# Two mixer phases of a transformer kernel take their inputs without the norm's root; the root meets each job's sums on the vector engine

## What is computed

```python
def rms_norm(x, gain, eps=1e-6):
    return x * lax.rsqrt(jnp.mean(x * x, axis=-1, keepdims=True) + eps) * gain

for l in range(2):
    x = x + 0.5 * swiglu(rms_norm(x, ffn1_norm[l]), ...)          # width 2816
    proj = rms_norm(x, mix_norm[l]) @ w_in[l]                     # 3328 columns
    y_rwkv = rwkv7_group(proj[..., :1792], ...)                   # p = p + mu * (p[t-1] - p[t]) first
    y_ret = retnet_group(proj[..., 1792:])                        # q, k rotary; v; gate silu(g)
    x = x + jnp.concatenate([y_rwkv, y_ret], -1) @ w_out[l]
    x = x + 0.5 * swiglu(rms_norm(x, ffn2_norm[l]), ...)
```

## Time and profile before

| | |
|---|---|
| median of 3 runs | 1433.2 us (1430.12 to 1433.49) |
| the profiled execution | 1431.56 us, of which its span 1429.7 us |
| PE busy | 1372.6 us, 96% |
| DVE busy | 986.9 us, 69% |
| ACT busy | 780.0 us, 55% |
| mean granted TensorE clock | 0.994 of full |

### The profile page before, as it was taken

The page is one execution under the profiler, slowest core; times in us unless marked ns, Lnnn a source line. Parts: engine busy times, 40 slices in busy tenths (PEclk is TensorE's granted clock), DMA queues, the critical chain, the costliest instruction groups (busy, mean ns, idle before and its releaser), DMA issues.

```text
span 1429.7 us, 28173 instructions
## 1 busy us (share of the span) xinstructions
PE 1372.6 (96%) x10866; PEld 1184.4 (83%) x10866; DVE 986.9 (69%) x1543; ACT 780.0 (55%) x1296; POOL 9.4 (1%) x23
## 2 busy tenths in 40 slices
PE   7998999999999999999999999999999999999997
PEld 7986887878888889877788887888879987788886
DVE  6977628877666677667766667766677855866665
ACT  6456546766555566335655555554565633655454
POOL 0000000000000000000000000000000000000000
PEclk9999999999999999999999999999999999999999
DMA  8732463145555554203565554655545401465551
GB/s 294 291 122 74 169 226 121 60 149 205 190 192 191 177 177 156 82 4 121 185 206 180 181 195 161 201 194 196 180 155 194 141 14 55 156 219 176 192 192 58
DMA packets 62789, 229.82 MB, mean 161 GB/s; under 512 B 7008, under 2 KB 7264, under 8 KB 62448
## 3 DMA queue, kind: packets, MB, share of 16 engines
q1 hardware_dynamic: 60912, 220.23, 45.8%
q0 software_dynamic: 1792, 8.37, 1.6%
HBM read 227.53 MB, written 1.05 MB: 160 GB/s over the span
## 4 chain that ended last, share of the span: by engine, by line
PE 83%; DVE 8%; ACT 6%; issue 2%; DMA 0%; DVEq 0%; SPq 0%; ACTq 0%
PE PS L793 23%; PE PS L1114 21%; PE PS L1134 16%; PE PS L1116 11%; DVE out_operands L2058 1%; PE PS L772 1%; PE PS L1322 1%; PE PS L1328 1%; DVE w_lo L2036 1%; PE PS L782 1%; DVE x_res L1962 1%; DVE w_lo L2318 1%; PE PS L1290 1%; ACT arena L1495 1%; PE PS L859 1%
## 5 line engine op out<-in xcount | busy, mean ns | idle before, releaser
L1114 PE MATMUL PS<-hT_both,w_hi 128*128 128x512 f32 x1376 | 489.9, 399 | 4.2 <-DVE w_lo L2318 4.2
L1116 PE MATMUL PS<-hT_both,w_lo 128*128 128x256 f32 x1376 | 386.1, 281 | 0.0
L1114 PEld LDWEIGHTS PS<-hT_both,w_hi 128*128 128x128 f32 x1376 | 258.5, 188 | 69.2 <-issue 3.4
L1116 PEld LDWEIGHTS PS<-hT_both,w_lo 128*128 128x128 f32 x1376 | 259.8, 189 | 3.0
L793 PE MATMUL PS<-hT_both,w_hi 128*128 128x256 f32 x1392 | 255.3, 286 | 2.3 <-DVE w_lo L2036 1.2
L793 PEld LDWEIGHTS PS<-hT_both,w_hi 128*128 128x128 f32 x1392 | 217.5, 192 | 6.5 <-issue 5.2
L2318 DVE TENSOR_TENSOR w_lo<-weight_ring,w_hi 128x1024 fp32r<-128x1024 f32 x176 | 207.1, 1218 | 2.4 <-ACT w_hi L1740 2.4
L793 PE MATMUL PS<-hT_both,w_lo 128*128 128x256 f32 x696 | 196.9, 283 | 0.0
L2324 DVE TENSOR_TENSOR w_lo<-weight_ring,w_hi 128x1024 fp32r<-128x1024 f32 x88 | 107.8, 1225 | 111.3 <-ACT w_hi L1749 111.3
L1740 ACT ACTIVATE w_hi<-weight_ring 128x1024 fp32r<-128x1024 f32 x176 | 175.4, 1045 | 0.0
L2036 DVE TENSOR_TENSOR w_lo<-weight_ring,w_hi 128x1024 fp32r<-128x1024 f32 x107 | 125.8, 1219 | 48.0 <-ACT w_hi L1518 47.8
(11 more groups left out here) (309 smaller groups left out, 1820.9 us busy)
## 6 DMA issues: line engine op xcount, KB each, us to landing
weight_ring<-in_stream SPq DMA_DIRECT2D x411, 512.0 KB, 4.4
norm_gain<-in_gains_in POOLq DMA_DIRECT2D x8, 512.0 KB, 4.2
consts<-in_csts POOLq DMA_DIRECT2D x1, 1864.0 KB, 9.4
arena<-in_taps_in SPq DMA_DIRECT2D x4, 384.0 KB, 3.4
arena<-in_bias_in POOLq DMA_DIRECT2D x1, 1152.0 KB, 12.4
x_res<-in_x_in SPq DMA_DIRECT2D x2, 512.0 KB, 3.7
lora<-in_lora_in POOLq DMA_DIRECT2D x2, 512.0 KB, 3.8
x_out<-yT SPq DMA_DIRECT2D x2, 512.0 KB, 2.7
```

Source lines behind the costliest of these rows:

```text
L1114: pe.matmul(PS[:, b, :], Wh[:, u, k, :], HT2[:, k], start=(k == 0), stop=(k == KT - 1), skip_group_check=True)
L1116: ins = pe.matmul(PS[:, b, 0:T], Wl[:, u, k, :], Hh[:, k, :], start=False, stop=(k == KT - 1), skip_group_check=True)
```

## The change

Mixers become "late" phases too. `late(n)` holds for them, so the seam into a mixer writes `x * gain` after each addition, and roots come behind the copies. PE makes the row of roots after J(0), in bank 7. In the mixer every sum but the two by token (J(9), J(10)) is multiplied by `root_row` on DVE as it leaves PSUM (`rooted`), in place of ACT's copy; ACT's copies of J(9) and J(10) take the root as their scale, and the gate's silu runs on SBUF behind DVE. In all late phases the first 128 tokens' root now comes before ACT's copies of the transposed inputs, the second's after them. In feed-forwards the PE waits for the gate's and the up projection's low parts one by one. In the even layer `fill(s)` stands ahead of `values(s - 2)`, and the sum of squares ahead of row k = 5.

```diff
-        ROOTS_AT = SPLIT_END + NTT * D + D
+        ROOTS_AT = ARENA - 2 * T - NTT
...
-            return n < len(PHASES) and PHASES[n][0].startswith("ffn")
+            return n < len(PHASES) and (PHASES[n][0].startswith("ffn") or PHASES[n][0] == "mix")
...
+            def row_of_roots(n, b):
+
+                pe.wait_ge(sem("roots_spread"), NTT * (late_before(n) + 1))
+                for t in range(NTT):
+                    ins = pe.matmul(PS[:, b, t * P:(t + 1) * P], cst("ones"), root_diag[:, t, :],
+                                    start=True, stop=True)
+                ins.then_inc(sem("root_row_made"), 1)
...
                     if s + 1 < n:
                         scores(s + 1)
+                    fill(s)
                     if s >= 2:
                         values(s - 2)
-                    fill(s)
...
-                    if k == 6:
+                    if k == 5:
                         pe.wait_ge(sem("convsq_made"), 1)
...
-                        if i == 0:
-                            pe.wait_ge(sem("gu_lo"), 2 * f0 + part + 1)
+                        pe.wait_ge(sem("gu_lo"), turns(it, 2 * FLOOP, 2 * (f0 + i) + part + 1))
...
                 J(0)
+                row_of_roots(n, 7)
                 J(1)
...
+            def late_root(n, t):
+                act.wait_ge(sem("x_made"), x_made_at(n - 1) + 2 * t + 2)
+                done.wait(done(act.activation(squares, X[:, t, :], ACT.Square, accum_out=stat[:, t:t + 1])))
...
-                act.activation(flat(qR), job_made(jb0, 7), ACT.Copy).then_inc(sem("job_out"), 1)
                 split_to(SPLIT["mix"][2][8])
...
-                act.activation(flat(kR), job_made(jb0, 8), ACT.Copy).then_inc(sem("job_out"), 1)
                 for n in (9, 10):
-                    act.activation(Vret[:, n - 9, :], job_made(jb0, n), ACT.Copy).then_inc(sem("job_out"), 1)
+                    split_to(SPLIT["mix"][2][n])
+                    act.wait_ge(sem("job_out"), jb0 + n)
+                    act.activation(Vret[:, n - 9, :], job_made(jb0, n), ACT.Copy, scale=stat[:, n - 5:n - 4])\
+                       .then_inc(sem("job_out"), 1)
...
                     act.preload_act_table_set("natural_log_exp_and_others")
+                    late_root(n, 0)
                     hT_split(n)
-                    late_roots(n)
+                    late_root(n, 1)
...
+                def rooted(n, dst):
+
+                    dve.wait_ge(sem("job_made"), jb0 + n + 1)
+                    dve.wait_ge(sem("root_row_copied"), late_before(ph) + 1)
+                    dve.tensor_tensor(dst, PS[:, job_bank("mix", n), :].rearrange("p (a t) -> p a t", a=2),
+                                      rep(root_row, 2), ALU.mult).then_inc(sem("job_out"), 1)
...
                     if n:
                         dve.wait_ge(sem("shift_made"), 7 * l + n)
+                    rooted(n, r[:, :, 1:T + 1])
+                    dve.wait_ge(sem("job_out"), jb0 + n + 1)
...
                 split_for(9)
+                rooted(7, qR)
                 dve.wait_ge(sem("decay_exp"), l + 1)
...
                 k = done(dve.tensor_tensor(flat(en), flat(en), flat(kh), ALU.mult))
                 done.wait(k)
 
+                rooted(8, kR)
...
+                dve.wait_ge(sem("job_out"), jb0 + 11)
+                rooted(11, gret[:, 0:2, :])
                 dve.tensor_tensor(flat(qW), flat(qR), cst("QW"), ALU.mult)
...
                     ins.then_inc(sem("st_masked"), 1)
+                rooted(12, gret[:, 2:4, :])
```

More of the change, by code:

```diff
@@ L1119, in gate_up @@
                     if i == 0:
[L1120 to L1124, removed]
+                        row_of_roots(n, 3)
                 def down(i, start, stop):
@@ L1141, in step @@
                 def step(i, it=None):
-                    if i:
-                        pe.wait_ge(sem("gu_lo"), turns(it, 2 * FLOOP, 2 * (f0 + i + 1)))
                     if f0 + i >= SS:
                         pe.wait_ge(sem("act_made"), turns(it, FLOOP, f0 + i - SS + 1))
-                    gate_up(i)
+                    gate_up(i, it)
                     if i == 0:
@@ L1490, in rstd, with root_row_copied @@
                        .then_inc(sem("rstd_made"), 1)
[L1492 to L1499, removed]
+            def root_row_copied(n, b):
+                act.wait_ge(sem("root_row_made"), late_before(n) + 1)
+                act.activation(root_row, PS[:, b, 0:T], ACT.Copy).then_inc(sem("root_row_copied"), 1)
+            def late_root(n, t):
+                act.wait_ge(sem("x_made"), x_made_at(n - 1) + 2 * t + 2)
+                done.wait(done(act.activation(squares, X[:, t, :], ACT.Square, accum_out=stat[:, t:t + 1])))
+                done.wait(done(act.activation(stat[:, 6 + t:7 + t], stat[:, t:t + 1], ACT.Ln,
+                                              scale=1.0 / D, bias=eps[:])))
+                act.activation(stat[:, 4 + t:5 + t], stat[:, 6 + t:7 + t], ACT.Exp, scale=-0.5)\
+                   .then_inc(sem("rstd_made"), 1)
             def hT_split(n):
@@ L1791, in ffn @@
                 act.preload_act_table(ACT.Silu)
-                act.wait_ge(sem("root_row_made"), late_before(n) + 1)
-                act.activation(root_row, PS[:, 3, 0:T], ACT.Copy).then_inc(sem("root_row_copied"), 1)
+                root_row_copied(n, 3)
                 for i in range(SS):
@@ L1805, in mixer @@
                 act.wait_ge(sem("const_loaded"), CONSTS)
[L1807 to L1813, removed]
+                root_row_copied(ph, 7)
                 split_to(SPLIT["mix"][2][1])
@@ L1818, in mixer @@
                 act.activation(sgd[:, :], wg[:, 1, :], ACT.Sigmoid).then_inc(sem("lora_in"), 1)
-                raw_copy(1)
-                raw_copy(2)
+                split_to(SPLIT["mix"][2][2])
                 act.wait_ge(sem("lora_made"), 3 * l + 1)
@@ L1830, in mixer @@
                 ins.then_inc(sem("a_made"), 1)
-                raw_copy(3)
+                split_to(SPLIT["mix"][2][3])
                 act.wait_ge(sem("lora_made"), 3 * l + 3)
@@ L1836, in mixer @@
                 for n in range(4, 7):
-                    raw_copy(n)
+                    split_to(SPLIT["mix"][2][n])
+                    act.wait_ge(sem("job_made"), jb0 + n - 1)
                 split_to(SPLIT["mix"][2][7])
@@ L1869, in gate_made @@
                 def gate_made(n):
-                    act.activation(flat(gret[:, 2 * n - 22:2 * n - 20, :]), job_made(jb0, n), ACT.Silu)\
-                       .then_inc(sem("job_out"), 1)
+                    split_to(SPLIT["mix"][2][n])
+                    act.wait_ge(sem("job_out"), jb0 + n + 1)
+                    g = flat(gret[:, 2 * n - 22:2 * n - 20, :])
+                    act.activation(g, g, ACT.Silu)
                 tok_copied(0)
@@ L1955, in added_to_x @@
                 factor = 1.0
-                if late(n):
+                if PHASES[n][0].startswith("ffn"):
                     dve.wait_ge(sem("roots_spread"), NTT * (late_before(n) + 1))
```

4 lines of the change are left out of this document (2 added, 2 removed).

## The result

The changed kernel takes 1450.47 us (median of 4 runs, 1447.8 to 1453.41) beside 1431.66 us for the kernel before (4 runs, 1426.54 to 1433.49): a ratio of 1.014 with a 95% interval of 1.012 to 1.016. It is slower, as forecast, but by some 19 us and not by 6, and above the range of 1432.0 to 1442.5.

A forecast was written before the change was run, and what follows sets the result against it. PE, busy 96% of the span, was taken as the bound, so any new standstill is paid in full. Terms -1.8 - 4.8 - 1.2 + 1.1 + 10.0 + 0.7 + 2.0 = +6.0 us on 1431.56 gave 1437.6, range 1432.0 to 1442.5.

The forecast's parts named there:

- Seams into the mixers, -1.8: Two seams into mixers, 9.98 and 9.13 us before, come down to a feed-forward seam's 8.65: gain 1.3 + 0.5 us.
- Feed-forward starts, -4.8: At four feed-forward starts, PE's eight waits for low gate parts (4.2 us) go: -4.8 us, between -4.2 and -5.0.
- Even layer, -1.2: Even layer: earlier squares remove the wait for L2065, -1.3 us; taps ahead of values win about nothing; net -1.2.
- Row of roots, +1.1: PE's four added 128x128 instructions after J(0), 0.55 us from start to start: +1.1 us for two mixers.
- ACT's splits start 1.6 us later behind that root, and J(1)'s tiles still come 1 to 2 us early.: Mixer start on ACT: splits delayed 1.6 us by the second root, J(1)'s tiles still early, so no added PE wait.
- The new wait at the rotation, +10.0: PE waits at each mixer's rotation for kR, made late in DVE's line: 4.9 to 5.0 us each, bounds 4.0 and 5.7.
- The rotated k, +0.7: DVE multiplies J(11) before the products ending in ret_qk_made, so PE gets the rotated k 0.35 us later per mixer.
- The clock, +2.0 (ends 0 and 4): PE's 5 us standstills at the rotations likely bring the lower clock: +2.0 us over two mixers, ends 0 and 4.
- +1.0 us for each mixer: Lower-clock cost behind each rotation's standstill, taken from the 0.85 us by which the second mixer's seam ran shorter.
- Rival C: Longer lower-clock stretch after the rotation wait, or root delaying ACT's copies in six seams: +11.6 us, 1443.2; 13%.
- Rival A: Rotation wait hidden, kernel faster at 1425.6 us; decided by whether work from J(6) to kR is under 16.8 us; 8%.

The follow-up runs named there:

- the best version: Kernel before with only the feed-forwards' edits and the even layer's squares ahead of row k = 5, mixers unchanged, taps in place: 1423.13 us, ratio 0.9949.
- both places mended: Changed kernel with ACT's splits ahead of the root row's copy and kR's multiplication directly behind qR's: 1429.85 us, ratio 0.9982.
- The first experiment: Changed kernel with ACT's splits of the mixer's tiles 2 to 5 put back ahead of its root row copy: 1444.05 us, ratio 1.0082.
- the second to fourth experiments: Changed kernel with kR's multiplication behind qR's, 1437.59 us; that plus ACT's splits first, 1429.85; splits first and J(10) ahead of the rotation, 1428.24.
- the mixer mended: Changed kernel with splits first, kR behind qR, J(11)'s multiplication behind the sum PE awaits, even layer as before: 1428.03 us, ratio 0.9974.

## Why the prediction was right in sign and wrong in size

Its steps, in its order, with what the changed kernel's trace and the runs showed:

- **Seams into the mixers, -1.8.** The first went from 9.98 to 8.64 us, as the feed-forward seam had said. The second went to 9.82 and not to 8.65: the clock fell near its end, as in only one other of the fourteen such seams traced here. Together -0.7; with 8.65 and the 10 us that a seam of before mostly takes it would be more.
- **Feed-forward starts, -4.8.** Measured -6.5 over four. The mechanism is right, the size was off twice: a listed wait of 0.61 us costs 0.85, and the edits take off some 0.3 us a layer besides the waits.
- **Even layer, -1.2.** Measured 0.0, which is the best of the seven traces with both edits. The squares bring -1.1 by themselves and -1.6 in the best version, about the -1.3 of the working; the taps, worked out at about nothing, give it back or more through the clock.
- **Row of roots, +1.1.** About right: with both places mended, the stretch that holds it is 0.43 us longer than before (15.88 against 15.45 us from the last pass of the seam's product to L1178, L1176 before).
- **"ACT's splits start 1.6 us later behind that root, and J(1)'s tiles still come 1 to 2 us early."** This is the step that failed. I counted the root ahead of the splits and not the copy of the root row, which the change puts ahead of them as well and which waits for PE. The splits start 4.8 us after the root's end and not right behind it, PE stands 2.81 us, and from the last pass of the seam's product to the mixer's next stage (L1176 before) the mixers lose 4.8 and 3.5 us, some 7.4 in all without the row of roots: 5.6 of standing, nearly all the rest at the lower clock behind it in the first mixer. The first experiment gives 6.4 us for it in whole kernels. It isn't the whole miss: with this mended the kernel still takes 1444.05 us, above the range, by the terms of the clock below.
- **The new wait at the rotation, +10.0.** Measured 9.4 us of standing, and 4.87 and 4.88 us from that stage to the rotation: +9.75. The step is right: kR left DVE in the order and with the durations that the working used. Its sum has a slip: 560.9 and 20.5 make 581.4 and not 581.7, which would have given a wait of 4.6.
- **The rotated k, +0.7.** Measured +1.15 (0.58 and 0.57), the wait itself 0.41.
- **The clock, +2.0 (ends 0 and 4).** Measured +4.9 behind the two rotations alone (2.25 and 2.66): the step "+1.0 us for each mixer", read from a seam, was less than half of it. This is the second step that failed, a term mis-sized. Besides this the clock fell once more at 1223 us (0.50 to 1226; 2.7 us with a stand of 0.81 ahead of it), in the second seam and in the even layer. The fall near the end of the second mixer is also in two of the other six kernels with the root inside, and in none of the seven without.

These terms make +19.6 us, with the odd layer's -3.4 some +16.2; 0.4 of the 16.6 is spread over the mixers. The odd layer's part is luck of these two executions; the medians, which hang less on a single one, differ by 18.8. Rival C came closest (1443.2), though through clock and delayed copies in the seams: the copies were not delayed, the splits were. Its clock cost of 4 was near the measured 4.9. Rival A's point of decision was right: once kR is there before PE, as in the second to fourth experiments, the wait and its clock go together.

## What to carry to other kernels

When an edit removes a helper's call, list everything that the helper did before its first wait: here the copy that was no longer needed carried the split that PE needed next. A new producer should be placed by its consumer's time, not by its kinship with others: one multiplication moved past four products was worth 13 us, and either engine's order could mend it. Price a standstill of PE by the matmuls behind it as well; and where two edits cover the same wait, one of them is nearly the whole gain.

## What the runs showed of the hardware that was not expected

- At the rotation a standstill of PE of 2.33 us was followed by 1.7 us of loss to the lower clock, one of 4.72 us by 1.7 to 2.6: where the clock falls, the shorter wait isn't much cheaper. It doesn't always fall: behind 2.3 us it did at both rotations and in ten of fourteen seams.
- In the even layer no single standstill was over 1.31 us, and the clock was still 0.50 behind the four of them; with 0.56 in the place of 1.31, and the taps between the waits, it stayed at 1.00.
- PE stands for nothing that the profile shows, 0.5 to 1.8 us at a time, at one to three places of each mixer. At the same instruction it was 1.53 us in the kernel before and 1.80 in the best version, whose mixers are the same code. For differences of 1 us in a mixer a single trace doesn't tell the edit from it. In the traces of three kernels (the one before, the one with both places mended and the one with the mixer mended), these stands fall where the instruction queue loads its blocks of 16,384 bytes every 3.4 to 5.0 us; elsewhere these loads lie 6.8 us or more apart; whether they cause the stands no run shows.
